# Hybrid decoder trunk, one core: the head norms of q and k done a chunk at a time, their order on the engines changed, and constant matmuls at the start

## The reference, cut to what matters

```
xn = rmsnorm(h, mix_norm[i])
u = xn @ w_in[i]                      # q 1024 | k 256 | v 256 | lx | lg | ga | gb, 1024 each
q = rmsnorm(q per head of 64, q_norm[i]);  k = rmsnorm(k per head of 64, k_norm[i])
y_a = sliding_window_attention(q, k, v, bias, mask, sinks[i])     # scores times 64 ** -0.5
y_b = rg_lru_branch(lx, lg, ...)
h = h + (sigmoid(ga) * (y_a @ w_proj_attn[i]) + sigmoid(gb) * (y_b @ w_proj_lru[i])) @ w_out[i]
h = h + ffn(rmsnorm(h, ffn_norm[i]))  # dense SwiGLU in layer 0, top 2 of 8 experts in layer 1
h = h + sigmoid(rmsnorm(h, ple_norm[i]) @ ple_gate_w[i]) * (p[i] @ ple_proj_w[i])
```

## Time and profile before

| | us |
|---|---|
| median of 3 runs | 1785.7 |
| lowest and highest | 1784.58 and 1787.78 |
| profiled execution, its own time | 1791.94 |
| profiled execution, span of its records | 1790.0 |

### The profile page before, as it was taken

How to read it: one execution, slowest core, us unless ns; L and a number is a source line. 1 busy time by engine, 2 the same in 40 slices (tenths; PEclk the granted TensorE clock), 3 DMA queues, 4 the chain that set the end, 5 groups by cost and what they waited for, 6 DMA issues and landing times. The chain is left out here.

```text
span 1790.0 us, 27179 instructions
## 1 busy us (share of the span) xinstructions
PE 1694.1 (95%) x10162; PEld 1302.1 (73%) x10163; DVE 1090.3 (61%) x1690; ACT 886.0 (49%) x1339; POOL 19.9 (1%) x51
## 2 busy tenths in 40 slices
PE   7899899999999999897999999999999999999988
PEld 5788899999997888896565665656655556656557
DVE  7696876665677796865464545555446454455536
ACT  6577544433355678434454544444434454444434
POOL 3000000000000000000000000000000000000000
PEclk9999999999999999998999999999999999999999
DMA  8333362644543433433999978999879999699961
GB/s 312 142 123 126 136 224 109 253 158 158 220 147 135 146 150 106 165 137 132 377 420 420 421 321 349 420 420 421 361 317 418 416 419 402 275 418 422 420 280 66
DMA packets 61883, 485.98 MB, mean 271 GB/s; under 512 B 6832, under 2 KB 9152, under 8 KB 10944
## 3 DMA queue, kind: packets, MB, share of 16 engines
q1 hardware_dynamic: 61584, 484.09, 67.5%
q10 hardware_dynamic: 176, 0.15, 0.1%
HBM read 483.15 MB, written 1.07 MB: 271 GB/s over the span
## 5 line engine op out<-in xcount | busy, mean ns | idle before, releaser
L2054 DVE TENSOR_TENSOR w_lo<-raw,w_hi 128x1024 fp32r<-128x1024 f32 x336 | 396.1, 1222 | 241.2 <-ACT w_hi L957 234.4
L957 ACT ACTIVATE w_hi<-raw 128x1024 fp32r<-128x1024 f32 x336 | 336.3, 1050 | 183.9 <-DMA raw<-in_moe_w 183.3
L476 DVE TENSOR_TENSOR w_lo<-raw,w_hi 128x1024 fp32r<-128x1024 f32 x236 | 283.4, 1220 | 111.9 <-ACT w_hi L471 111.0
L1109 PE MATMUL work<-x_r,w_hi 128*128 128x256 f32 x1024 | 299.5, 293 | 15.4 <-DVE w_lo L476 11.5
L1110 PE MATMUL work<-x_r,w_hi 128*128 128x256 f32 x1024 | 291.8, 285 | 0.0
L1111 PE MATMUL work<-x_r,w_lo 128*128 128x256 f32 x1024 | 291.4, 285 | 0.0
L471 ACT ACTIVATE w_hi<-raw 128x1024 fp32r<-128x1024 f32 x236 | 241.1, 1048 | 68.9 <-PE work L1111 29.7
L1109 PEld LDWEIGHTS work<-x_r,w_hi 128*128 128x128 f32 x1024 | 198.4, 194 | 24.7 <-issue 18.6
L1109 PE MATMUL work<-w_hi,bias_r 128*128 128x512 f32 x448 | 185.9, 415 | 25.1 <-DVE w_lo L2054 17.8
L1441 PE MATMUL acc<-raw,bias 128*64 128x512 f32 x896 | 204.6, 598 | 0.0
L1110 PEld LDWEIGHTS work<-x_r,w_hi 128*128 128x128 f32 x1024 | 198.6, 194 | 1.0 <-issue 0.8
(11 more groups left out here) (340 smaller groups left out, 2596.9 us busy)
## 6 DMA issues: line engine op xcount, KB each, us to landing
raw<-in_moe_w SPq DMA_DIRECT2D x336, 1024.0 KB, 10.0
raw<-in_mix_w SPq DMA_DIRECT2D x33, 2048.0 KB, 7.8
raw<-in_dense_w SPq DMA_DIRECT2D x21, 2048.0 KB, 8.0
raw<-in_ple_w SPq DMA_DIRECT2D x4, 2048.0 KB, 10.0
raw<-in_mix_w SPq DMA_DIRECT2D x4, 512.0 KB, 7.1
areaK<-in_ple_p SPq DMA_DIRECT2D x2, 1024.0 KB, 9.6
hT<-in_xT SPq DMA_DIRECT2D x4, 256.0 KB, 6.1
gate_b<-bias_line SPq DMA_DIRECT2D x1, 1024.0 KB, 5.8
```

Of the source, the lines that this page charges most:

```text
L476: eng.tensor_tensor(unit(w_lo, g), raw_part(g), unit(w_hi, g).bitcast(F32), ALU.subtract).then_inc(split_ok, 1)
L957: act.activation(w_hi[n % UNITS_HELD][:, :], heavy_quarter(where, j), ACT.Copy).then_inc(m_hi_ok, 1)
L1109: pe.matmul(out, stat[0], move[0], start=start, stop=False, skip_group_check=True)
L2054: dve.tensor_tensor(w_lo[u][:, :], heavy_quarter(where, n % HEAVY_C), w_hi[u][:, :].bitcast(F32), ALU.subtract).then_inc(m_split, 1)
```

## The change

ACT squares both halves of a chunk one after the other, DVE sums, inverts and applies both, and ACT takes the roots of both in one instruction: three turns a layer in place of six. The weight of q's norm is multiplied into k's once, with the factor 64 ** -0.5 (scores are products of q and k, both weights act on the same 64 elements), so q is no longer multiplied by a weight. The sequence of units, `renorm` and `renorm_lo` between the turns is written out anew. In layer 1 TensorE sums the squares of h after all of chunk 0 as in layer 0. ACT's square root table is loaded ahead of the rounding of a unit (of three in layer 0), not right before the roots. The root of k's heads is taken after the evacuation of lx 0. The decays are made at g == 22, not at g == 2. Before its first product TensorE does 26 matmuls of 128 columns with `ones` and `ident`, whose result nothing reads. The first rounding beyond chunk 0 (`to(UNITS_HELD + 4)`) is left to the mixer's own sequence.

```diff
+WARM = 26
-            def norm_root(n):
+            def norm_root(n, after_table=None):
...
                 act.activation(small[:, 65:66], eps_col, ACT.Sqrt)
+                if after_table is not None:
+                    after_table()
                 act.wait_ge(summed, n + 1)
...
+            def qk_square(l, c):
+                n = 512 if c < 2 else 256
+                if c:
+                    act.wait_ge(qk_summed, 3 * l + c)
+                for tt in range(TT):
+                    wait_full(act, l, "qkv", c, tt)
+                    if c == 2:
+                        act.activation(v_sb[:, tt, :], bank_of(l, "qkv", c, tt)[:, 256:512], ACT.Copy,
+                                       scale=rinv_col[:, tt:tt + 1])
+                    act.activation(sqs[:, tt, 0:n], bank_of(l, "qkv", c, tt)[:, 0:n], ACT.Square,
+                                   scale=rinv_col[:, tt:tt + 1]).then_inc(qk_squared, 1)
+
+            def qk_root(l, c):
+                h = 8 if c < 2 else 4
+                act.wait_ge(qk_summed, 3 * l + c + 1)
+                act.activation(head_rms[:, :, 0:h], head_sum[:, :, 0:h], ACT.Sqrt, bias=eps_col,
+                               scale=1.0 / HD).then_inc(qk_rooted, 1)
+
             def qk_norm(l):
+                g = phase_q[(l, "mix")]
+                hi.to(g + 5)
+                norm_root(3 * l, lambda: hi.to(g + (6 if l else 8)))
+                hi.to(g + 10)
+                act.wait_ge(rinv_ok, 3 * l + 1)
+                renorm(l, range(0, 4))
+                qk_square(l, 0)
+                renorm(l, range(4, 8))
+                qk_root(l, 0)
+                hi.to(g + 13)
+                qk_square(l, 1)
+                hi.to(g + 14)
+                qk_root(l, 1)
+                hi.to(g + 17)
+                qk_square(l, 2)
...
                     evacuate(l, name, j, dst)
+                    if g == 0:
+                        qk_root(l, 2)
...
-            hi.to(UNITS_HELD + 4)
...
-                        if c == 0 and q == (1 if l else 3):
+                        if c == 0 and q == 3:
                             norm_root(3 * l)
...
             pe.wait_ge(ident_ok, 1)
+            for _ in range(WARM):
+                pe.matmul(misc[:, 0:P], ones[:, :], ident[:, :], start=True, stop=True)
...
-                step(dve.tensor_scalar(row[:, R_Q:R_Q + DEPTH * HD], row[:, R_Q:R_Q + DEPTH * HD], HD ** -0.5, None, ALU.mult))
+                step(dve.scalar_tensor_tensor(out=row[:, R_K:R_K + DEPTH * HD], in0=row[:, R_Q:R_Q + DEPTH * HD], scalar=HD ** -0.5,
+                                              in1=row[:, R_K:R_K + DEPTH * HD], op0=ALU.mult, op1=ALU.mult))
...
+            def qk_sum(l, c):
+                n = 512 if c < 2 else 256
+                h = n // HD
+                dve.wait_ge(qk_squared, 6 * l + 2 * c + 2)
+                dve.tensor_reduce(head_sum[:, :, 0:h], sqs[:, :, 0:n].rearrange("p t (h d) -> p t h d", h=h),
+                                  AX_X, ALU.add).then_inc(qk_summed, 1)
+
+            def qk_inverse(l, c):
+                h = 8 if c < 2 else 4
+                dve.wait_ge(qk_rooted, 3 * l + c + 1)
+                step(dve.reciprocal(head_inv[:, :, 0:h], head_rms[:, :, 0:h]))
+                step.settle()
+                for tt in range(TT):
+                    step(dve.tensor_scalar(head_inv[:, tt, 0:h], head_inv[:, tt, 0:h], rinv_col[:, tt:tt + 1], None, ALU.mult))
+                step.settle()
+
+            def scaled_heads(l, c, tt, dst):
+                h = 8 if c < 2 else 4
+                ps = bank_of(l, "qkv", c, tt)[:, 0:h * HD].rearrange("p (h d) -> p h d", h=h)
+                rb = head_inv[:, tt, 0:h].unsqueeze(2).to_broadcast([P, h, HD])
+                taken(dve.tensor_tensor(dst, ps, rb, ALU.mult), l, "qkv", c, tt)
+
+            def normed_q(l, c):
+                for tt in range(TT):
+                    scaled_heads(l, c, tt, q_tok[:, tt, 512 * c:512 * c + 512].rearrange("p (h d) -> p h d", h=8))
+                for tt in range(TT):
+                    wait_taken(dve, l, "qkv", c, tt)
+                dve.sem_inc(qk_normed, 2)
+
+            def normed_k(l):
+                for tt in range(TT):
+                    scaled_heads(l, 2, tt, k_dup[:, tt, :, 0, :])
+                gain = row[:, R_K + HD * l:R_K + HD * l + HD].unsqueeze(1).to_broadcast([P, KV_HEADS, HD])
+                for tt in range(TT):
+                    kd = k_dup[:, tt, :, :, :]
+                    wait_taken(dve, l, "qkv", 2, tt)
+                    step(dve.tensor_tensor(kd[:, :, 0, :], kd[:, :, 0, :], gain, ALU.mult))
+                step.settle()
+                for tt in range(TT):
+                    kd = k_dup[:, tt, :, :, :]
+                    dve.tensor_copy(kd[:, :, 1, :], kd[:, :, 0, :]).then_inc(qk_normed, 1)
+
             def qk_norm(l):
+                g = phase_q[(l, "mix")]
+                lo.to(g + (6 if l else 8))
+                norm_root(3 * l)
+                lo.to(g + 8)
+                renorm(l, range(0, 4))
+                lo.to(g + 9)
+                qk_sum(l, 0)
+                renorm(l, range(4, 8))
+                lo.to(g + 10)
+                qk_inverse(l, 0)
+                normed_q(l, 0)
+                lo.to(g + 11)
+                renorm_lo(l, range(0, 4))
+                lo.to(g + 12)
+                renorm_lo(l, range(4, 8))
+                lo.to(g + 13)
+                qk_sum(l, 1)
+                lo.to(g + 14)
+                qk_inverse(l, 1)
+                normed_q(l, 1)
+                lo.to(g + 16)
+                qk_sum(l, 2)
+                lo.to(g + 17)
+                qk_inverse(l, 2)
+                normed_k(l)
...
-                    if l == 0 and g == 2:
+                    if l == 0 and g == 3 * KT - 2:
                         decays()
...
-            lo.to(UNITS_HELD + 4)
```

More of the change, by code:

```diff
@@ L251, in trunk @@
         rms_col, rinv_col = small[:, 84:84 + TT], small[:, 88:88 + TT]
+        head_sum, head_rms, head_inv = (small[:, o:o + 16].rearrange("p (t h) -> p t h", t=TT) for o in (0, 16, 48))
         def squares_of(n):
@@ L768, in renorm @@
                     act.activation(xn_hi[:, k, :], xnT[:, k, :], ACT.Copy).then_inc(xn_rounded, 1)
-            def qk_norm(l):
[L771 to L793, removed]
```

## The result

The changed kernel takes 1764.05 us (median of 4 runs, 1762.81 to 1766.13); before, measured beside it, takes 1785.41. The medians lie 21.4 us apart; the measured ratio is 0.9868, with a 95% interval of 0.9849 to 0.9886, which is 23.6 us less, 20 to 27. Forecast were 26 us and 1760 us, in a range of 1756 to 1771. Its profiled execution took 1762.81 us, its span is 1760.9.

A forecast was written before the change was run, and what follows sets the result against it. TensorE, busy 1694.10 of 1790.00 us, was taken as the bound, so only its idle or slow-clock time pays. Layer 0's 12.3 and layer 1's 13.8 us make 26.1 off the median 1785.7: 1760 us, range 1756 to 1771.

The forecast's parts named there:

- rival B: ACT or DVE late at several joints, gaps of 4 to 10 us in all: 1764 to 1770 us; chance 0.18.
- Rival A: Constant matmuls at the start all slow and do not pay: 3.0 us lost against the sum, 1762.6 us; chance 0.10.
- Rival C: Part of the gain given back later, in the expert stage; half of it lost, 1773 us; chance 0.06.
- Part 1: TensorE's start: constant matmuls end at 10.05, chunk 0 takes 10.9 us and not 13.4; 2.0 us gained.
- Layer 0 in all: Layer 0 up to the turning of q and k, at 62.6 where it was 74.94: 12.3 us gained.
- Layer 1: Layer 1's q/k/v stage without a stop of TensorE: 45.0 us where it was 58.8, 13.8 gained.
- The walk of the queues: ACT's and DVE's steps in q/k/v timed from trace prices, 0.05 us a handover, against when TensorE wants them.
- the tightest joints: Five joints with under 1 us to spare: remainders 9, 10 and 11, the first bias copy, bank 0.
- The wait on the fourth chunk: Layer 0, unit 12: weights land at about 38.3, ACT rounds by 39.4, DVE comes at 41.4; 2 us cover hides it.
- The table load: ACT's load ahead of unit 5's rounding: 1.28 us without drain; with a 1.38 us drain, remainder 10 1.0 us late.
- Rival D: DVE bounds the attention units, each of 32 turns taking longer; at 1 us a turn 1792 us; chance 0.03.
- Decays at nothing: About 3.8 us of small DVE steps moved to where DVE waits, costed at nothing; without that cover, up to 3.8.

The follow-up runs named there:

- second pair of profiles: Kernel before and changed kernel, both run again without an edit: 1786.3 us (ratio 0.9987) and 1762.9 us (ratio 0.9854 to before).
- the run with 26 us more at the head: Changed kernel with 144 constant matmuls in place of 26: 1788.9 us, ratio 1.0008 to before.
- the old turns: Kernel before with constant matmuls, late sums in layer 1 and late decays, keeping its six turns and order of units: 1790.2 us, ratio 1.0019 to before.

## Why the prediction was right

The median lies 4 us above the forecast of 1760 us, inside the range, and the faster side was given 0.95 (its parts, the forecast, A, B and C, add up to 0.97). The time alone would not tell the forecast from rival B, whose 1764 to 1770 us begin at the median; the profile does, step by step:

- Part 1. Forecast 2.0 us. The constant matmuls start at 2.04, not 1.91, and the first product comes at 10.70 and 9.26 in the two profiles of the changed kernel (9.26 to 10.70 over all with 26 of them in the changed kernel's variants, forecast 10.05). Against the run without them the gain is 0.6 and 1.7 us, and 1.2 on average over all profiles. This is the term that was sized too large; the time until the upper level is reached differs from one execution to the next, and I had taken it from one. Rival A, all of them slow, did not happen.
- Layer 0 in all: forecast 12.3, measured 11.3 and, in the second pair of profiles, 11.4. In the first pair 0.8 of the missing 1.0 is part 1, some 0.15 us the q/k/v products (96 in 22.0 us, forecast 21.85). In the second, part 1 gave 2.2 us (chunk 1 at 20.96 for 23.19), and the miss is elsewhere: before itself went from chunk 1 to the turn in 50.7 us, not 51.3, as less of it behind the third flip was at the lower level (60.53 to 73.93, where the first profile has 60.60 to 74.94); the changed kernel lost some 0.35 us at remainder 10 and the third flip, which TensorE met just as they were ready.
- Layer 1: forecast 13.8 and a stage of 45.0 us; measured 13.7 and 45.1.
- The walk of the queues held within 0.6 us at every joint read above. The slack that it named at the tightest joints was too small: with 2.8 us a layer more work put in by the weight of q, only 0.9 us a layer came out. Rival B did not happen: no gap of 1 to 2 us stands at any joint.
- The wait on the fourth chunk was there, 2.42 us at ACT, and hidden, as forecast.
- The table load: 20.45 is the next start, 1.29 us after 19.16. The drain that the Trainium skill (ScalarE: Activation LUTs, What ACT_TABLE_LOAD costs) adds does not show here either, and remainder 10 was not late.
- Rival C: the run with 26 us more at the head cost 26.0 us; nothing is given back. Rival D: turns of the attention take as long as before (470.9 us between the stages, 470.7, and 208.5 from the turn of layer 1 to the first gather, 209.1).
- Decays at nothing: so in one profile.

Sum of the head: 24.8 and 25.0 us in the two pairs of profiles, forecast 26.1. From the time the gain reads 23.6 with 20 to 27 as its interval, and 26 in the longer second comparison (0.9854). The 4 us between the forecast and the first median are thus some 1.2 us of the head, and for the rest the spread of a stage that no edit touches.

Not settled by a run of its own: how the 0.69 us before the turn could be saved, and how much the earlier table load gains in layer 0 (in layer 1 nothing, as shown above).

## What to carry to other kernels

Write down for each unit when the bound engine wants it and when the feeding engine has it, with prices from the trace; here that put every joint read above within 0.6 us. The order of work on the feeders, undone alone, cost 15.8 us of the two stretches, where the merging of instructions cost 3.8. A wait that is taken away is only gained if the next one in line has slack: late sums and constant matmuls gave 1.3 and 0 us in the kernel before, and 6.7 and about 1 once the order was right. When the time of a kernel differs by 10 us from one execution to the next, read small steps from the stretch that they change, not from the total.

## What the runs showed of the hardware

The lower clock level behind an idle stretch doesn't follow from its length alone. TensorE's second half of chunk 2 in layer 0, 24 matmuls, took 5.6 us behind 2.44 and 2.81 us of idle time in the two profiles of before, but 7.2 behind 2.57 in the run with merged turns and the order of before. The granted clock of these stretches says the same, 1.00 and 0.76 (the second profile of before, then that run):

```profile
42.71:48.28 5.57, 5.57 (x24) 4.62 (x25) 5.13 (x10) 1.16 (x3) 0.00 (x0) 1.00 0.64 209
```

```profile
41.36:48.53 7.17, 7.17 (x24) 5.76 (x25) 6.59 (x12) 2.45 (x4) 0.00 (x0) 0.76 0.78 285
```

Behind the same 3.52 us in layer 1, lx 2 and 3 took 7.3 us in before (granted clock 0.77) and 8.5 with the old turns (0.64). At the start, the same 52 records of constant matmuls took between 7.2 and 8.7 us from one execution to the next.

The granted clock of a profile does not show the slow start. In before the first matmuls start some 0.43 us apart, from 9.55 to 14.38, and the column reads 1.00; the same spacing behind the idle 8.58 us of the merged run reads 0.50. At the start only the spacing tells the level.

```profile
9.55:14.38 4.83, 4.83 (x12) 3.76 (x12) 4.44 (x8) 4.72 (x8) 4.83 (x7) 1.00 1.07 442
```

```profile
564.45:567.00 2.55, 2.55 (x6) 2.07 (x7) 2.55 (x3) 0.92 (x1) 0.00 (x0) 0.50 0.40 84
```
